# Fused conformer, MLP and attention kernel: the second pointwise product and the first MLP chunk by block of 128 tokens, and the last modulation vector as dot products inside the MLP

## The chip, the cores and the metric

One Trainium2 chip, one of its cores. The metric is the device time of one execution in microseconds. A difference of under about 0.2% (2 us) can't be told from no change for this kernel, as its three runs of before already lie 1.8 us apart.

## The reference, cut to what matters

The part of the program that is changed lies in the first block: conformer convolution, gated residual, modulated norm, squared-relu MLP, gated residual. x has 256 tokens of 1,024 channels; the MLP is 4,096 wide.

```python
mod = (silu(c) @ w_mod + b_mod)                      # six vectors of 1,024
sh1, s1, g1, sh2, s2, g2 = jnp.split(mod, 6, axis=-1)
# conformer_conv ends in:  u = silu(layer_norm(u)); y = u @ w_pw2 + b_pw2
xl = xl + g1 * y
hf = rms_norm(xl, norm2_g) * (1.0 + s2) + sh2
xl = xl + g2 * (jnp.square(jax.nn.relu(hf @ w1)) @ w2)
# second block: two attention layers with their own MLPs, then the last norm
```

The kernel numbers the six vectors in its own way: 0 and 1 are scale and shift of the first norm, 2 is g1, 4 and 3 are scale and shift of the second norm, 5 is g2.

## The kernel before

All products run in three passes of fp32r: each weight tile is split into a high part `hi` (ScalarE, L612) and a low part `lo` (VectorE, L1068), each activation likewise into `xh` and `xl` (or `gh` and `gl`), and TensorE adds high*high, low*high and high*low.

Weights come as one stream of units of 1 MB each, in a fixed order that `plan_units` writes out. SyncE's queue (SP) issues all of them, in that order, each into one of six slots of `raw` and `scratch`. A unit is issued when the unit six places before it has been consumed: a split unit when its `lo` is made, a modulation unit when its dot products or its products on TensorE are done. SP is one queue: an instruction that waits there holds back all that are behind it. The split parts have three slots, so `hi` of a unit waits until the product three units before it is done.

A modulation vector comes in four units (quarters) that are consumed in one of two ways. As dot products (`dots`, L1137), VectorE multiplies two halves of the unit with a row that holds silu(c), and sums. In the other way TensorE multiplies (`quarters`, L1757), ScalarE copies the result (`quarter_copy`, L669) and TensorE adds it up, into columns (`column_sums`, L1776) for scale and shift, or into a row (`row_sum`, L1788 and L1789, then `row_copy`, L677) for g2. `DOTS` says which units are dot products. g1, made of dot products, is a column; SP writes it to DRAM (L553) and reads it back as a row on all partitions (L556).

Names in what follows: the units in question are, in stream order, **28** and **29** (third quarters of vectors 4 and 3), **30** and **31** (their last quarters), **32** and **33** (the two halves of w1's first chunk), then in the kernel before the four quarters of g2, and then w1's second chunk. **24** and **27** are the last two units of the second pointwise product (pw2), whose splits are s=10 and s=11 in the code; the splits of 32 and 33 are s=12 and s=13.

The order of work on each engine is written out by hand; each engine runs its list in order. Before the change the stretch in question is, on VectorE: `lo` of 24, dot products of 29, `lo` of 27, dot products of 30 and 31, `lo` of 32, the gated residual in four pieces (block of 128 tokens by half of the channels; L1316 multiplies, L1319 adds), norm of block 0 (L1329), `lo` of 33, norm of block 1, the four low parts of the activation (L1278). The sum of squares is ScalarE's (L625), the root is GpSimd's (L1014, L1017). TensorE runs pw2 (`token_major` and `last_pw2`), then the four quarters of g2 with their row sums and, between them, the transposes of blocks 0 and 1 (`mid_T`, L1955), and then the MLP. Each of the MLP's eight chunks is a w1 product of 96 matmuls with the weights stationary and 256 tokens moving (L2007), whose result is the hidden layer already transposed, and a w2 product of 96 matmuls of 512 columns (L1652).

Of the kernel before, what the change touches and what calls it, by code (L numbers as in the profile page):

```python
# [14 lines left out]
P = 128  # L15
# [171 lines left out]
MOD_BANKS = [5] * GROUPS + [7, 6, 2, 3] + [0] * 4  # L187
SUM_AT = [(6, 0)] * GROUPS + [(3, QUARTER)] + [(6, 0)]
ROW_UNITS = (8, 9, 10, 11)
COLUMN_UNITS = ((None, 0), (None, 1), (None, 2), (None, 3), (4, 5), (6, 7))  # L190
# [5 lines left out]
def copies(m):  # L196

    return m + 1
# [25 lines left out]
ROWS = ("b_mod5", "b_pw2", "b_pw1a", "b_pw1g")  # L224
# [6 lines left out]
V_END = 10 * KT  # L231
# [5 lines left out]
def build(nc, stream, x, p_t, vectors, rows, rel, consts, dft_tables, taps, tap_bias, out):  # L237

    ctx = ExitStack()
    with ctx:  # L240
# [55 lines left out]
        def carve(table, start=0, limit=16512):  # L296
            views, at = {}, start
            for name, size in table:
# [6 lines left out]
                     ("stage", 4 * QUARTER), ("sel", P), ("sel1", 1), ("csb", KT * 32), ("g1", D), ("crow", D), ("dot", 2 * len(DOT_UNITS)), ("gate", KT),  # L305
# [18 lines left out]
        sq = one["yb"][:, 0:KT * SEQ].rearrange("p (f t) -> p f t", f=KT)  # L324
        hid1 = one["yb"][:, 0:NB * MLP_CHUNK].rearrange("p (b c) -> p b c", b=NB)
# [55 lines left out]
        gate_dram = nc.dram_tensor("gate_dram", (D,), F32, kind="Internal").ap()  # L381
# [8 lines left out]
        row_sums row_evac midT_ps mid_done mid_hi mid_lo xT_ps xh_ready xl_ready pw2_ps res_step relu_done  # L390
# [30 lines left out]
        def stage_free(eng, m):  # L421

            if m < 4:
                return
            old = m - 4
            if old in ROW_UNITS:
                eng.wait_ge(S["row_sums"], ROW_UNITS.index(old) + 1)
            else:
                eng.wait_ge(S["col_sums"], [old in g for g in COLUMN_UNITS].index(True) + 1)

# [10 lines left out]
        def nval(n, b):  # L441

            return 2 * WHOLE.index(n) + b + 1

# [55 lines left out]
        def _(sp):  # L500
# [31 lines left out]

            sp.dma_start(vec, vectors).then_inc(S["in_vec"], 16)
# [18 lines left out]
            sp.wait_ge(S["gate_done"], 1)  # L552
            sp.dma_start(gate_dram.rearrange("(p j) -> p j", p=P), one["gate"]).then_inc(S["gate_dma"], 16)  # L553
            sp.wait_ge(S["wave_ps"], CHUNKS)
            sp.wait_ge(S["gate_dma"], 16)
# [1981 lines left out]
```

## Time and profile before

| | |
|---|---|
| median of 3 runs | 1026.15 us (1024.49 to 1026.32) |
| profiled execution, its own time | 1025.7 us |
| its span, first to last instruction | 1023.8 us |
| TensorE busy (share of the span) | 992.0 us (97%) |
| VectorE, ScalarE busy | 618.1 us (60%), 503.9 us (49%) |
| mean granted TensorE clock | 0.993 of full |

The span is what the engines' rows add up to; the profiled execution's own time is 1.9 us longer. TensorE is busy nearly all the time, so that what counts is where it isn't, and what it waits for there.

### The profile page before, as it was taken

To read this page: it belongs to the slowest core of one execution; us is meant where nothing else is said; L and a number is where in the kernel's file an instruction comes from. 1 tells how busy PE (TensorE), PEld (TensorE's weight loads), DVE (VectorE), ACT (ScalarE), POOL (GpSimd) and SP (SyncE) were. 2 spreads that over 40 slices of the span, in tenths; PEclk is the share of its full clock that TensorE was granted. 3 is DMA by queue.
4 is the path that set the end of the run, shared out by engine and by line. 5 is a ranking of instruction groups with operands and counts; after the bars stand their busy time and mean duration, and the time that the engine had idled before them with its cause. 6 is when DMAs were issued, how large, how long until landed. Compare 5 with 4: busy or idle time off the path is not lost.

```text
span 1023.8 us, 13497 instructions
## 1 busy us (share of the span) xinstructions
PE 992.0 (97%) x5626; PEld 837.5 (82%) x5626; DVE 618.1 (60%) x748; ACT 503.9 (49%) x628; POOL 25.0 (2%) x47
## 2 busy tenths in 40 slices
PE   8999899999998999999999999999999999999996
PEld 6665689999987999878888888889987788888885
DVE  5786935444448649865455455664895654545465
ACT  4445365455454547644444444653664644443453
POOL 0000000000000000010000000100000100000010
PEclk9999899999999999999999999999999999999999
DMA  9987886654525443245555456435323555555531
GB/s 334 415 307 278 331 349 234 205 200 165 198 70 193 176 152 130 71 165 206 203 170 203 170 200 221 158 133 201 124 83 125 195 206 170 200 186 185 199 110 41
DMA packets 30934, 196.07 MB, mean 192 GB/s; under 512 B 3731, under 2 KB 5832, under 8 KB 9880
## 3 DMA queue, kind: packets, MB, share of 16 engines
q1 hardware_dynamic: 30874, 195.22, 52.6%
q8 instruction: 44, 0.72, 0.3%
q14 instruction: 16, 0.13, 0.0%
HBM read 194.14 MB, written 2.04 MB: 192 GB/s over the span
## 4 chain that ended last, share of the span: by engine, by line
PE 80%; DVE 12%; issue 3%; ACT 3%; DMA 2%; POOL 0%; SPq 0%; DVEq 0%; POOLq 0%; ACTq 0%
PE ps L1652 56%; PE ps L2007 9%; PE ps L2063 5%; DVE lo L1068 3%; ACT hi L612 1%; DMA scratch<-stream 1%; PE ps L1757 1%; PE ps L2311 1%; PE ps L2193 1%; PE ps L2147 1%; DVE scratch L1444 1%; DMA h<-x 1%; DVE scratch L1510 1%; DVE scratch L1461 1%; PE ps L2214 0%
## 5 line engine op out<-in xcount | busy, mean ns | idle before, releaser
L1068 DVE TENSOR_TENSOR lo<-raw,hi 128x2048 fp32r<-128x2048 f32 (+5 forms) x140 | 310.3, 2219 | 232.1 <-ACT hi L612 232.1
L612 ACT ACTIVATE hi<-raw 128x2048 fp32r<-128x2048 f32 (+4 forms) x140 | 263.8, 1888 | 143.1 <-PE ps L1652 110.1
L1652 PE MATMUL ps<-hi,xh 128*128 128x512 f32 (+2 forms) x704 | 275.1, 391 | 10.0 <-DVE xl L1109 4.4
L1652 PE MATMUL ps<-lo,xh 128*128 128x512 f32 (+2 forms) x704 | 269.2, 382 | 0.0
L1652 PE MATMUL ps<-hi,xl 128*128 128x512 f32 (+2 forms) x704 | 268.9, 382 | 0.0
L1652 PEld LDWEIGHTS ps<-hi,xh 128*128 128x128 f32 x704 | 132.2, 188 | 45.0 <-issue 11.1
L1652 PEld LDWEIGHTS ps<-lo,xh 128*128 128x128 f32 x704 | 132.1, 188 | 25.1
L1652 PEld LDWEIGHTS ps<-hi,xl 128*128 128x128 f32 x704 | 132.4, 188 | 22.6
L1652 PE MATMUL ps<-hi,gh 128*128 128x512 f32 (+2 forms) x328 | 125.2, 382 | 0.0
L1652 PE MATMUL ps<-lo,gh 128*128 128x512 f32 (+2 forms) x328 | 124.6, 380 | 0.0
L1652 PE MATMUL ps<-hi,gl 128*128 128x512 f32 (+2 forms) x328 | 124.5, 380 | 0.0
L2007 PE MATMUL ps<-xh,hi 128*128 128x256 f32 x256 | 72.6, 284 | 0.8 <-DVE xl L1278 0.8
L2007 PE MATMUL ps<-xh,lo 128*128 128x256 f32 x256 | 72.4, 283 | 0.0
L2007 PE MATMUL ps<-xl,hi 128*128 128x256 f32 x256 | 72.4, 283 | 0.0
L1652 PEld LDWEIGHTS ps<-hi,gh 128*128 128x128 f32 x328 | 61.6, 188 | 11.5 <-issue 0.7
L1652 PEld LDWEIGHTS ps<-lo,gh 128*128 128x128 f32 x328 | 61.6, 188 | 11.4
L1652 PEld LDWEIGHTS ps<-hi,gl 128*128 128x128 f32 x328 | 61.6, 188 | 10.8
L2063 PE MATMUL ps<-xh,hi 128*128 128x256 f32 x192 | 55.3, 288 | 0.9 <-DVE lo L1068 0.7
L2063 PE MATMUL ps<-xl,hi 128*128 128x256 f32 x192 | 54.3, 283 | 0.0
L2063 PE MATMUL ps<-xh,lo 128*128 128x256 f32 x192 | 54.3, 283 | 0.0
L2007 PEld LDWEIGHTS ps<-xh,hi 128*128 128x128 f32 x256 | 49.1, 192 | 1.7 <-issue 1.3
L2007 PEld LDWEIGHTS ps<-xl,hi 128*128 128x128 f32 x256 | 49.1, 192 | 0.2
(257 smaller groups left out, 1062.8 us busy)
## 6 DMA issues: line engine op xcount, KB each, us to landing
raw<-stream SPq DMA_DIRECT2D x142, 1024.0 KB, 4.8
scratch<-stream SPq DMA_DIRECT2D x22, 1024.0 KB, 8.9
raw<-stream SPq DMA_DIRECT2D x4, 1020.0 KB, 5.0
raw<-stream SPq DMA_DIRECT2D x4, 896.0 KB, 4.9
raw<-stream SPq DMA_DIRECT2D x2, 864.0 KB, 4.5
raw<-stream SPq DMA_DIRECT2D x2, 768.0 KB, 5.1
raw<-stream SPq DMA_DIRECT2D x2, 680.0 KB, 5.1
h<-x SPq DMA_DIRECT2D x2, 512.0 KB, 5.3
```

What stands on the lines that cost most here:

```text
L612: nc.scalar.activation(hi[:, u["s"] % SPLIT_SLOTS, 0:n], raw_of(u, n), ACT.Copy).then_inc(S["hi_done"], 1)
L1068: nc.vector.tensor_tensor(lo[:, slot, first:n], raw_of(u, n)[:, first:n], hi[:, slot, first:n].bitcast(F32), ALU.subtract).then_inc(S["lo_ ...
L1444: nc.vector.scalar_tensor_tensor(out=work[b], in0=r[:, k, :], scalar=iw[:, b, head:head + 1], in1=in1, op0=ALU.mult, op1=ALU.add).then_inc ...
L1461: nc.vector.match_replace(work[b], top8[:, b, :], work[b], TAKEN).then_inc(S["topk_step"], 1)
L1510: nc.vector.tensor_scalar(pm[b][:, hh, :], pm[b][:, hh, :], row_inv[:, c:c + 1], None, ALU.mult).then_inc(S["m_norm"], 1)
L1652: ins = nc.tensor.matmul(out, l, r, start=start and i == 0, stop=stop and i == 2, skip_group_check=skip)
L1757: ins = nc.tensor.matmul(ps[32 * j:32 * j + 32, MOD_BANKS[m], 0:QUARTER], csb[:, k, :], w[:, k, :], start=step == 0, stop=step == 1)
L2007: ins = nc.tensor.matmul(out_, w[:, k, cs], a[:, kk, :], start=(kk == 0 and c % 2 == 0 and i == 0), stop=(kk == KT - 1 and i == 2), skip_g ...
L2063: ins = nc.tensor.matmul(ps[:, bank + c // 2, (c % 2) * SEQ:(c % 2 + 1) * SEQ], w[:, k, cs], a[:, kk, :], start=(kk == 0 and c % 2 == 0 an ...
L2147: nc.tensor.matmul(ps[:, bank, at % 512:at % 512 + nk], qT[0:QK, hh, b * P:(b + 1) * P], kT[0:QK, hh, 0:nk], start=True, stop=False, skip_ ...
L2193: ins = nc.tensor.matmul(ps[:, bank, dst], w, sbt[:, hh, src], start=False, stop=True, skip_group_check=True)
L2311: ins = nc.tensor.transpose(ps[:, 6 + b, k * P:(k + 1) * P], hid2[:, b, k * P:(k + 1) * P], ident)
```

## The change

1. `DOTS` loses the last quarters of vectors 4 and 3 (units 30 and 31, now products on TensorE with column sums, the seventh group of `COLUMN_UNITS`) and gains all four of g2. g2's quarters move from ahead of the MLP's second chunk into chunks 1 to 4, one in each, as dot products; the result goes through DRAM like g1's. Row sums, row copies and their constants go away.
2. SP: the write of g1 no longer stands right ahead of its read. Units 28 to 31 are issued between the two.
3. pw2's last two units run as a `closing_pair`: block 0, then block 1, and ahead of its last six matmuls TensorE runs the quarters of 30 and 31 and the transposes of block 0.
4. Residual, sum of squares (now in halves), norm, scale and shift and the splits of the activation are written block by block. The first four channel groups of a block are ScalarE's, the last four VectorE's (`mid_second`).
5. The first w1 chunk is token major: 48 matmuls of 512 columns, block 0 and then block 1, with `mid_T(1)` between. Its result isn't transposed, so that eight transposes of the hidden layer (`first_hidden_T`) are added in the second chunk.

```diff
-DOTS = {(0, 0), (0, 1), (0, 2), (0, 3), (2, 0), (2, 1), (2, 2), (2, 3), (4, 2), (3, 2), (4, 3), (3, 3)}
+DOTS = {(0, 0), (0, 1), (0, 2), (0, 3), (2, 0), (2, 1), (2, 2), (2, 3), (4, 2), (3, 2), (5, 0), (5, 1), (5, 2), (5, 3)}
...
-    mod(5, 0, 1, 2, 3)
     for j in range(MLP_CHUNKS + 1):
         if 0 < j < MLP_CHUNKS:
             add("w1", j, [4, 4], MLP_CHUNK)
+        if 0 < j <= GROUPS:
+            mod(5, j - 1)
...
+            gate_write(0)
+            at, end = end, units_of("w1", 0)[0]["index"]
+            weights(UNITS[at:end])
+            gate_read(0, one["g1"])
...
+            def mid_high(b):
+
+                act.wait_ge(S["midT_ps"], b + 1)
+                if b == 0:
+                    act.wait_ge(S["pw2_ps"], 2)
...
+                sl = slice(b * P, (b + 1) * P)
+                for i in range(KT // 2):
+                    pair = slice(2 * i, 2 * i + 2)
+                    if i < 2:
+                        for f in (2 * i, 2 * i + 1):
+                            nc.scalar.activation(full[:, f, sl], ps[:, 4 + 2 * b, f * P:(f + 1) * P], ACT.Identity, scale=in_scale[:, KT + f:KT + f + 1],
+                                                 bias=in_shift[:, KT + f:KT + f + 1]).then_inc(S["mid_own"], 1)
+                        act.wait_ge(S["mid_own"], 4 * b + 2 * (i + 1))
+                    else:
+                        act.wait_ge(S["mid_full"], 4 * b + 2 * (i - 1))
+                    nc.scalar.activation(xh[:, pair, sl], full[:, pair, sl], ACT.Copy).then_inc(S["mid_hi"], 1)
+
+            mid_squares(0)
             feed(units_of("w1", 0)[1], 0)
-            squares(1, 0)
             quarter_copy(8)
...
             quarter_copy(9)
...
+            mid_high(0)
+            mid_squares(1)
+            mid_high(1)
...
+            mid_residual(0, 0)
+            mid_residual(0, 1)
+            mid_norm(0)
+            mid_residual(1, 0)
+            scale_columns(7)
+            shift_columns(7)
+            dve.wait_ge(S["scale_done"], 2 * GROUPS)
+            dve.wait_ge(S["shift_done"], 2 * GROUPS)
+            mid_second(0)
+            mid_low(0, 0, 1, 2, 3)
+            mid_residual(1, 1)
+            feed(units_of("w1", 0)[1], 0)
+            mid_norm(1)
+            mid_second(1)
+            mid_low(1, 0, 1, 2, 3)
             for j in range(MLP_CHUNKS):
                 feed(last_of("w1", j))
+                if 0 < j <= GROUPS:
+                    dots(5, j - 1)
...
+            def last_quarters():
+
+                quarters(8)
+                quarters(9)
+                mid_T(0)
...
+            closing_pair(units_of("pw2")[2:4], xh, xl, lambda ins: ins.then_inc(S["pw2_ps"], 1), KT - 1, last_quarters)
+            column_sums(6)
...
+            def mid_waits(u, b):
+
+                pe.wait_ge(S["mid_lo"], 4 * b + 2 * u["part"] + 2)
...
+            token_major(units_of("w1", 0), xh, xl, [slice(0, MLP_CHUNK)], lambda b, i: ps[:, b, :],
+                        done=lambda ins: ins.then_inc(S["w1_ps"], 1), waits=mid_waits, together=(2,), between=second_mid_T)
```

VectorE, from `lo` of unit 27 to the first low parts of the activation. Before:

```order
L1068 TENSOR_TENSOR lo<-raw,hi 128x2048
L1137 SCALAR_TENSOR_TENSOR raw,scratch<-raw,scratch 128x1024 x4
L1152 TENSOR_TENSOR scratch<-scratch 128x2
L1155 TENSOR_TENSOR scratch<-scratch 128x2
L1170 TENSOR_TENSOR scratch<-scratch 128x2
...
L1068 TENSOR_TENSOR lo<-raw,hi 128x2048
L1316 TENSOR_TENSOR xs<-ps,scratch 128x512
L1319 TENSOR_TENSOR h<-xs,h 128x512
...
L1329 TENSOR_SCALAR xs<-h,rstd 128x1024
L1068 TENSOR_TENSOR lo<-raw,hi 128x2048
L1329 TENSOR_SCALAR xs<-h,rstd 128x1024
```

And in the changed kernel, from `lo` of unit 32 (L1106 is the line of all `lo`, L1357 and L1360 are the residual's two steps, L1370 is the norm, L1189 to L1208 the scale and shift columns, L1376 `mid_second`, L1386 `mid_low`):

```order
L1106 TENSOR_TENSOR lo<-raw,hi 128x2048
L1357 TENSOR_TENSOR xs<-ps,scratch 128x512
...
L1370 TENSOR_SCALAR xs<-h,rstd 128x1024
L1357 TENSOR_TENSOR xs<-ps,scratch 128x512
L1360 TENSOR_TENSOR h<-xs,h 128x512
L1189 TENSOR_TENSOR scratch<-ps,scratch 128x2
...
L1376 TENSOR_SCALAR scratch<-ps,scratch 128x128 x4
L1386 TENSOR_TENSOR xl<-scratch,xh 128x2x128 x4
L1357 TENSOR_TENSOR xs<-ps,scratch 128x512
L1360 TENSOR_TENSOR h<-xs,h 128x512
L1106 TENSOR_TENSOR lo<-raw,hi 128x2048
L1370 TENSOR_SCALAR xs<-h,rstd 128x1024
```

The four dot-product instructions of units 30 and 31 are gone from here. Both `lo` of w1's first chunk keep their place in the list, the first ahead of every residual piece, the second now behind the last residual piece and behind all of block 0's activation.

SP, from the issue of g1's write. Before:

```order
L553 DMA gate_dram<-scratch 128x8
L556 DMA scratch<-gate_dram 128x1024
L515 DMA scratch<-stream 128x2048 x2
L515 DMA raw<-stream 128x2048 x4
```

And in the changed kernel:

```order
L537 DMA gate_dram<-scratch 128x8
L516 DMA scratch<-stream 128x2048 x2
L516 DMA raw<-stream 128x2048 x2
L543 DMA scratch<-gate_dram 128x1024
L516 DMA raw<-stream 128x2048 x2
L519 DMA gain<-row_final_g 128x1024
```

The read of g1 (0.5 MB) has moved behind units 28 to 31 and stands now right ahead of units 32 and 33.

## Rows read from the trace of the kernel before

**Rows 1.** Windows: busy time by engine, granted clock, DMA share and GB/s.
```profile
92.00:96.00 4.00, 4.00 (x52) 2.98 (x50) 1.08 (x4) 2.76 (x6) 0.00 (x0) 1.00 0.97 281
127.00:130.00 3.00, 3.00 (x26) 1.87 (x18) 2.29 (x2) 0.54 (x2) 2.16 (x2) 0.63 1.01 355
120.15:135.24 15.09, 11.42 (x91) 5.89 (x90) 9.72 (x13) 8.27 (x16) 2.93 (x4) 0.77 1.01 413
```

**Rows 2.** Timeline of TensorE, 119 to 136 us: start, time, engine, line, what.
```profile
119.76 0.39 PE L1652 MATMUL ps<-lo,xh 128*128 128x512 f32 x1
122.48 1.94 PE L1757 MATMUL ps<-scratch 128*32 128x256 f32 x16 [2.33 <-DMA scratch<-stream]
128.43 1.44 PE L1955 MATMUL ps<-table,xs 128*128 128x128 f32 x8
131.55 1.09 PE L1955 MATMUL ps<-table,xs 128*128 128x128 f32 x8
135.24 0.36 PE L2007 MATMUL ps<-xh,hi 128*128 128x256 f32 x1 [0.85 <-DVE xl L1278]
```

**Rows 3.** The chain that ended last, 140 us on: start, time, what.
```profile
141.22 0.43 PE ps L1788 x2
141.96 17.47 PE ps L2007 x144
159.43 10.91 PE ps L1652 x48
```

**Rows 4.** Timeline of VectorE, 103 to 131 us.
```profile
103.72 0.16 DVE L1152 TENSOR_TENSOR scratch<-ps,scratch 128x2 f32<-128x2 f32 x1
104.06 2.28 DVE L1068 TENSOR_TENSOR lo<-raw,hi 128x2048 fp32r<-128x2048 f32 x1
118.10 2.29 DVE L1068 TENSOR_TENSOR lo<-raw,hi 128x2048 fp32r<-128x2048 f32 x1 [1.38 <-ACT hi L612]
120.31 0.68 DVE L1316 TENSOR_TENSOR xs<-ps,scratch 128x512 f32<-128x512 f32 x1
122.36 0.69 DVE L1319 TENSOR_TENSOR h<-xs,h 128x512 f32<-128x512 f32 x1
126.28 2.29 DVE L1068 TENSOR_TENSOR lo<-raw,hi 128x2048 fp32r<-128x2048 f32 x1
129.28 0.75 DVE L1329 TENSOR_SCALAR xs<-h,rstd 128x1024 f32<-128x1024 f32 x1 [0.71 <-POOL rstd L1017]
```

**Rows 5.** Timeline of ScalarE: `hi` of unit 32, and the first pair.
```profile
116.15 1.92 ACT L612 ACTIVATE hi<-raw 128x2048 fp32r<-128x2048 f32 x1 [11.25 <-DMA raw<-stream]
132.68 1.02 ACT L745 ACTIVATE scratch<-ps,scratch 128x256 f32<-128x256 f32 x2 [0.61 <-PE ps L1955]
```

**Rows 6.** SP: timeline of its issues, then its waits (total, times, longest).
```profile
91.12 0.33 SPq L556 DMA_DIRECT2D scratch<-gate_dram  x1
106.37 4.82 SPq L515 DMA_DIRECT2D raw<-stream  x4
...
SPq L555 <- DMA gate_dram<-scratch: 6.3, 1, 6.3
```

**Rows 7.** Groups by form: busy, mean ns of one, idle before.
```profile
L631 ACT ACTIVATE scratch<-h 128x512 f32<-128x512 f32 x12 | 7.6, 631 | 9.2 <-DVE h L1357 4.9 <-DVE h L1374 4.3
L877 ACT ACTIVATE scratch<-ps,neg_max 128x128 f32<-128x128 f32 x12 | 4.3, 406 | 0.0
L967 ACT ACTIVATE gh<-ps 128x256 fp32r<-128x256 f32 x40 | 13.2, 381 | 65.9 <-PE ps L2311 65.9
L1564 DVE TENSOR_SCALAR scratch<-scratch,row_inv 128x128 f32<-128x128 f32 x10 | 2.1, 283 | 0.1
L1606 DVE TENSOR_TENSOR gl<-ps,gh 128x256 fp32r<-128x256 f32 x40 | 15.1, 420 | 28.5 <-ACT gh L967 28.5
L1137 DVE SCALAR_TENSOR_TENSOR raw<-raw,scratch 128x1024 f32<-128x1024 f32 x20 | 23.6, 1220 | 1.0 <-DMA raw<-stream 0.9
```

**Rows 8.** Timeline of VectorE in an MLP chunk.
```profile
186.14 2.29 DVE L1068 TENSOR_TENSOR lo<-scratch,hi 128x2048 fp32r<-128x2048 f32 x1 [5.71 <-ACT hi L612]
```

More of the change, by code:

```diff
@@ L324, in build @@
         sq = one["yb"][:, 0:KT * SEQ].rearrange("p (f t) -> p f t", f=KT)
+        full = one["u"].rearrange("p (k t) -> p k t", k=KT)
         hid1 = one["yb"][:, 0:NB * MLP_CHUNK].rearrange("p (b c) -> p b c", b=NB)
@@ L424, in stage_free @@
                 return
[L425 to L429, printed above, removed]
+            eng.wait_ge(S["col_sums"], [m - 4 in g for g in COLUMN_UNITS].index(True) + 1)
         NORMS = 3 + 3 * LAYERS + 1
@@ L759, in _, with mid_squares @@
             feed(units_of("w1", 0)[0], 0)
+            def mid_squares(b):
+                for c in range(2):
+                    if c == 0:
+                        act.wait_ge(S["res_step"], 3 * b + 2)
+                    else:
+                        act.wait_ge(S["h_ready"], hval(1, b))
+                    cs = slice(c * CHUNK, (c + 1) * CHUNK)
+                    nc.scalar.activation(xs[:, b, cs], h[:, b, cs], ACT.Square, scale=D ** -0.5,
+                                         accum_out=half_ss[:, 2 * b + c:2 * b + c + 1]).then_inc(S["sumsq"], 1)
@@ L1325, in _, with mid_residual @@
-            for b in range(NB):
-                if b:
-                    feed(units_of("w1", 0)[1], 0)
+            def mid_residual(b, c):
+                at = 2 * b + c
+                if at < 3:
+                    dve.wait_ge(S["pw2_ps"], at + 1)
+                else:
+                    product(dve, "pw2")
+                cs = slice(c * CHUNK, (c + 1) * CHUNK)
+                nc.vector.tensor_tensor(xs[:, b, cs], ps[:, at, :], one["g1"][:, cs], ALU.mult).then_inc(S["res_step"], 1)
+                rstep[0] += 1
+                dve.wait_ge(S["res_step"], rstep[0])
+                ins = nc.vector.tensor_tensor(h[:, b, cs], xs[:, b, cs], h[:, b, cs], ALU.add)
+                if c == 0:
+                    ins.then_inc(S["res_step"], 1)
+                    rstep[0] += 1
+                else:
+                    ins.then_inc(S["h_ready"], 1)
@@ new lines, in mid_low @@
+            def mid_low(b, *pairs):
+                sl = slice(b * P, (b + 1) * P)
+                for i in pairs:
+                    dve.wait_ge(S["mid_full"], 4 * (b + 1))
+                    dve.wait_ge(S["mid_hi"], KT // 2 * b + i + 1)
+                    pair = slice(2 * i, 2 * i + 2)
+                    nc.vector.tensor_tensor(xl[:, pair, sl], full[:, pair, sl], xh[:, pair, sl].bitcast(F32), ALU.subtract).then_inc(S["mid_lo"], 1)
+            dve.wait_ge(S["gate_dma"], 32)
+            mid_residual(0, 0)
@@ L1936, in pw2_waits @@
                     column_sums(5)
-            def last_pw2(b):
-                u = last_of("pw2")
-                pw2_waits(u, b)
-                wh, wl = parts(u)
-                sl = slice(b * P, (b + 1) * P)
-                for i, c in enumerate(halves):
-                    for k in range(u["kts"]):
-                        kk = u["k0"] + k
-                        ins = three(ps[:, 2 * b + i, :], xh[:, kk, sl], xl[:, kk, sl], wh[:, k, c], wl[:, k, c], start=False,
-                                    stop=kk == KT - 1)
-                    ins.then_inc(S["pw2_ps"] if 2 * b + i < 3 else S["used"], 1)
             def mid_T(b):
@@ L1989, in w2_product @@
                     used(ins, u)
-            for j in range(MLP_CHUNKS):
+            for j in range(1, MLP_CHUNKS):
                 if j >= 2:
```

207 lines of the change are left out of this document (92 added, 115 removed).

## The prediction

> **What bounds the kernel now.** I read the windows first: from 120.15 to 135.24 us, between the last matmul of pw2 and the first of the MLP, TensorE is busy for 11.42 of 15.09 us at a granted clock of 0.77 [rows 1], and none of it is work of the large products. Then the timeline of TensorE [rows 2]: the last pw2 matmul starts at 119.76 and is through at 120.0, a wait of 2.33 us for a DMA follows (the first quarter of g2), then quarters, row sums and transposes, and the first w1 matmul starts at 135.24 after a wait for VectorE. From there the chain is TensorE alone [rows 3]: 144 matmuls of 256 columns in 17.47 us (0.121 each), 48 of 512 columns in 10.91 us (0.227 each). The row sum and its step at 141.22 cost 0.74 us (the next piece starts at 141.96). So the first w1 chunk ends at 141.96 + 48 x 0.121 = 147.8, and behind it TensorE has no gap in the MLP. All that the change can win or lose lies between 120.0 and 147.8, and in what it adds to TensorE behind that.
>
> What sets the order in that stretch is not TensorE. ScalarE waits 11.25 us for unit 32 and starts `hi` at 116.15 [rows 5]; VectorE's `lo` follows at 118.10, the first residual piece at 120.31 [rows 4]. So all of the residual hangs on the landing of unit 32. The stream is in turn held by VectorE: SP issues unit 30 at 106.37 [rows 6], right when `lo` of unit 24 (104.06 + 2.28 = 106.34) [rows 4] has freed its slot.
>
> **Step 1, the landing of unit 32.** The wait for g1's write, 6.3 us on SP [rows 6], goes away, and units 28 and 29 can be issued somewhat earlier. I cost this at nothing: the next issue, unit 30, waits for `lo` of 24, and that `lo` waits for a column sum on TensorE (the scale column at 103.72) [rows 4], neither of which moves. But g1's read, which at 91.12 fell in idle time of the queues, now stands between 31 and 32. It is 0.52 MB in a stream that leaves no gap, for which I take the rate of the full stretch in rows 1, 413 GB/s: 1.25 us. The trace shows such reads dearer. With g1's read under way the rate is 281 GB/s over 4 us (92 to 96), 4 x (413 - 281) / 413 = 1.3 us lost beside its own 1.25, together 2.6, part of which is the start of the queue; with a gain row of the same size it is 355 over 3 us (127 to 130), 0.4 lost, together 1.7 [rows 1]. I take 1.9, nearer to the row inside a running stream; bounds 1.25 and 2.6. `hi` of 32 then starts at 118.05, `lo` at 120.0, the first residual piece at 122.2.
>
> The Trainium skill's page "DMA: Bandwidth & Descriptors" (Where 436 GB/s comes from) has the ports' ceiling at 435 GB/s and gives no penalty for a row that is read 128 times over. By it alone the read would cost 1.2 us and the sum below would be 0.7 lower; the two windows speak against it.
>
> **Step 2, TensorE up to the norm of block 0.** pw2's matmuls are the same in number. All but the last six (6 x 0.227 = 1.4) are done by 118.7, or 0.4 later, as block 0 alone needs `lo` of 27 sooner; the quarters of 30 and 31 take about 1.0 each at full clock (half of 1.94, which was at half clock) [rows 2]. TensorE is free at 121.1 and waits for the norm of block 0. On VectorE a residual piece takes 1.35 us (from 120.31 to the second piece's add, which ends at 123.05, it is 2.74 for two) [rows 4]: both are through at 124.95. Half a sum of squares is 0.63 on ScalarE [rows 7] and 0.1 more to read it out; GpSimd's small step, 0.3 by the usual size of such steps, and its root follow, for which VectorE waited 0.71 [rows 4]: about 1.75 in all; the norm takes 0.75 [rows 4]. The transposes can start at 127.5. TensorE has then been idle for 6.4 us, with pw2's last six matmuls queued behind the wait.
>
> **The clock.** In the trace 2.33 us of idleness were followed by half clock, 1.2 GHz: 16 quarter matmuls took 1.94, eight transposes 1.44 against 1.09 at full clock [rows 2]. After 6.4 us I expect half clock too: transposes to 128.8, six matmuls of 512 columns at twice 0.227 to 131.4, column sums to 132.2. At full clock all this would be 1.7 us shorter.
>
> The page "TensorE: Matmul & The Clock Gate" (Part 1, HAM oscillation) says that idleness between bursts puts the array back to half rate and that only sustained matmuls lift it again. The trace agrees for the fall. By that rule block 0's product, in pieces with waits between, might stay slow; that is a rival below, priced from rows.
>
> **Step 3, block 0's activation.** Behind the column sums VectorE makes the last scale and shift columns (0.34, from 103.72 to 104.06) [rows 4] and starts `mid_second` at 132.8. It and `mid_low` are not in the trace. For 128x128 with two operands I take 0.22 each, the nearest row (L1564, 0.283) less the usual overlap of 0.07; for 128x256 from L1606 (0.42) 0.34 each [rows 7]. Four and two: low parts for w1's first half at 134.5, all four at 135.1. The first w1 matmul thus starts at 134.55, hardly before the old 135.24. The half-product is 12 x 0.227 = 2.7, to 137.3.
>
> **Step 4, the second `lo`.** It was hidden under the transposes at 126.28 [rows 4]. Now it comes behind the last residual piece: 135.1 + 1.35 + 2.25 = 138.7. Block 0's second half waits 1.4 us for it and ends at 141.5. The norm of block 1 stands behind that `lo` and is done by some 140.2, hidden by this half.
>
> **Step 5, block 1.** Transposes 141.5 to 142.5. Nothing is left to cover the evacuation: ScalarE makes two 128x128 pieces and one 128x256 copy for each pair. At 0.33 to 0.4 and 0.38 [rows 7] a pair is 1.1 us; as a floor, half of the old pair's two (1.02 for two of 256 columns) [rows 5] with the copy gives 0.85, and as a ceiling the old pair unchanged, 1.6. Two pairs and one low part: 2.7, floor 2.2, ceiling 3.7. TensorE starts at 145.3, and 24 x 0.227 = 5.45 end the chunk at 150.8. The product itself is 10.9 instead of 11.5.
>
> **Step 6, the rest.** Eight transposes more in chunk 2: 1.0 at full clock [rows 2]. g2 costs VectorE 2 x 1.22 = 2.4 us in each of four chunks [rows 7]; they fall in the 5.7 us that VectorE is idle each chunk [rows 8]. Without this cover it would be up to 2.4 x 4 = 9.8. In the first of them `hi` and `lo` of w2's first unit (1.9 + 2.3) come behind the hidden transposes and have 5.8 us of w1's second half: enough, with 0.2 to 0.4 to spare after the copies. g2's write and read stand where SP has nothing urgent; all that is small at the start (one copy less) is nothing.
>
> **Sum.** 150.8 - 147.8 = 3.0, plus 1.0, is +4.0; I add 0.1 for the chance that the clock is back later. Against the profiled execution's own 1025.7 that is 1029.8; the median of the runs is 0.45 above it, so 1030.2.
>
> **Rivals.**
> - *The clock stays down through block 0's product.* For it: waits at 132.2 and 137.3 break up what TensorE has. Against: the old rise came while it did small pieces (0.63 mean in 127 to 130) [rows 1]. Block 0's halves would take 5.5 each instead of 2.7: the first ends at 140.0, past the second `lo`, the second at 145.5 instead of 141.5: 1034.
> - *The small terms fall low.* g1's read at its full rate (-0.65), six matmuls and what stands round them at full clock (-1.7), evacuation at its floor (-0.5): the first two together give 1027.9, all three 1027.3.
> - *The released SP decides (the other side).* If what paces the stream were g1's 6.3 us wait and not `lo` of unit 24, units 30 to 33 would land up to 6.3 earlier, and with them the residual: 1030.2 - 6.3 = 1023.9. It decides from a gain of 6.1 on. For it: VectorE's dot products of unit 28 had to wait for that load. Against: 106.37 follows 106.34 on the dot.
> - *A split in chunks 1 to 4 comes late* because the dot products stand ahead of `lo` units: each 0.5 us late in four chunks gives +2, 1032. Against: 5.7 us idle for 2.4 of work.
>
> **How the numbers follow.** My sum 0.52 (own range 1028.6 to 1032), clock down 0.13, small terms 0.18 (half of it above 1028.2), released SP 0.07, late splits 0.10. The range, 1027.4 to 1034, leaves out the released SP (0.07), half of the clock case (0.06), 0.03 of the small terms and 0.02 of the late splits. The bounds of step 1 and 5 alone (-0.65 to +0.7, -0.5 to +1.0) give 1029 to 1032. With 2 us as what can be told: slower by more 0.84 (all but half of the small terms and the released SP), within 0.09, faster 0.07.
>
> **What would show it.** Right: g1's read ahead of unit 32 and `hi` of 32 some 2 us later; TensorE idle for about 6 us ahead of block 0's transposes, then half clock; a wait of 1 to 2 us for `lo` inside block 0's product, one of 2 to 3 us ahead of block 1's; no gap in chunks 2 to 8. It would be wrong if unit 32 doesn't land later, if the first w1 matmul starts much before 134, or if gaps appear in the later chunks.

## The result, and the profile after

The changed kernel takes 1035.14 us, the median of four runs (1033.13 to 1037.01); the kernel before took 1026.13 beside it (1024.49 to 1026.32). The ratio is 1.0093, 95% interval [1.0081, 1.0105]: slower by 0.9%, where +0.4% was predicted. The predicted 1030.2 and its range, 1027.4 to 1034.0, are both too low. The profiled execution is the quickest of the four, 1033.13 us, with a span of 1031.3 (before 1023.8) and a mean granted clock of 0.990 (0.993). So 7.5 us of the difference can be read in the trace.

SP's timeline (start, time) has the issues where the prediction put them: units 30 and 31, g1's read, units 32 and 33.

```profile
106.90 0.80 SPq L516 DMA_DIRECT2D raw<-stream  x2
107.82 0.36 SPq L543 DMA_DIRECT2D scratch<-gate_dram  x1
108.22 3.50 SPq L516 DMA_DIRECT2D raw<-stream  x2
```

ScalarE's timeline has `hi` of unit 32 at 120.04, where [rows 5] has 116.15:

```profile
120.04 1.91 ACT L629 ACTIVATE hi<-raw 128x2048 fp32r<-128x2048 f32 x1 [14.61 <-DMA raw<-stream]
```

From the first of these issues it is now 13.14 us, before it was 9.78 [rows 5, 6]: the landing is 3.36 us later. The other 0.53 of the 3.89 is from the kernel's start (unit 30 is issued at 106.90 instead of 106.37, g1's write is 0.53 later too). The windows (columns as in [rows 1], GB/s last) show the stretch from the issue of unit 30 to `hi` of 32, before and then in the changed kernel; then, in the changed kernel, a slow stretch of the stream, and the stretch from the quarters to the first w1 matmul:

```profile
106.37:116.15 9.78, 9.78 (x45) 8.09 (x44) 9.30 (x15) 0.00 (x0) 0.00 (x0) 1.00 0.88 358
```

```profile
106.90:120.04 13.14, 12.88 (x59) 10.03 (x61) 4.77 (x8) 0.00 (x0) 0.00 (x0) 1.00 0.93 348
114.00:116.00 2.00, 2.00 (x10) 1.65 (x10) 0.00 (x0) 0.00 (x0) 0.00 (x0) 1.00 0.97 297
119.81:137.86 18.05, 7.35 (x56) 5.72 (x55) 9.60 (x18) 9.36 (x18) 0.86 (x2) 0.71 0.80 334
```

From the issue of unit 30 to `hi` of 32 the queues moved 358 GB/s x 9.78 us = 3.50 MB before, and now 348 x 13.14 = 4.57 MB. Of the 1.07 MB more the read is 0.52; the other 0.55 MB isn't the read's, so data from behind unit 32 moved before unit 32 was whole. A rate doesn't show that part (1.3 us at 413 GB/s).

From the quarters to the first w1 matmul TensorE is busy for 7.35 of 18.05 us, at 0.71 of its clock (before 11.42 of 15.09 at 0.77, [rows 1]). Its timeline, to be held against [rows 2]:

```profile
119.81 1.93 PE L1835 MATMUL ps<-raw,scratch 128*32 128x256 f32 x32
129.58 1.97 PE L2003 MATMUL ps<-table,xs 128*128 128x128 f32 x8 [7.83 <-DVE xs L1370]
131.20 0.78 PE L1728 MATMUL ps<-hi,xh 128*128 128x512 f32 x1
131.77 0.63 PE L1728 MATMUL ps<-hi,xl 128*128 128x512 f32 x1
...
133.91 1.08 PE L1854 MATMUL ps<-scratch 128*128 128x1 f32 x8
137.86 0.76 PE L1728 MATMUL ps<-hi,xh 128*128 128x512 f32 x1 [2.87 <-DVE xl L1386]
...
144.90 1.03 PE L2003 MATMUL ps<-table,xs 128*128 128x128 f32 x8
148.96 0.50 PE L1728 MATMUL ps<-hi,xh 128*128 128x512 f32 x1 [3.02 <-DVE xl L1386]
```

Three waits stand where [rows 2] has 2.33 and 0.85: 7.83 us for block 0's norm, 2.87 for its low parts, 3.02 for block 1's. Behind the first, TensorE works at half clock (1.2 GHz): eight transposes in 1.97, matmuls of 512 columns every 0.43 us. The granted clock is back at 1.00 from 134.2, is 0.50 again from 137.6, just ahead of the first w1 matmul, and 1.00 from 141.0. VectorE's timeline shows what they wait for:

```profile
121.98 2.29 DVE L1106 TENSOR_TENSOR lo<-raw,hi 128x2048 fp32r<-128x2048 f32 x1 [10.28 <-ACT hi L629]
124.19 0.68 DVE L1357 TENSOR_TENSOR xs<-ps,scratch 128x512 f32<-128x512 f32 x1
...
128.77 0.75 DVE L1370 TENSOR_SCALAR xs<-h,rstd 128x1024 f32<-128x1024 f32 x1 [1.84 <-POOL rstd L1055]
...
135.03 0.16 DVE L1189 TENSOR_TENSOR scratch<-ps,scratch 128x2 f32<-128x2 f32 x1 [4.17 <-PE ps L1854]
...
135.55 1.37 DVE L1376 TENSOR_SCALAR scratch<-ps,scratch 128x128 f32<-128x128 f32 x4
136.95 1.43 DVE L1386 TENSOR_TENSOR xl<-scratch,xh 128x256 fp32r<-128x256 f32 x4
...
139.62 2.28 DVE L1106 TENSOR_TENSOR lo<-raw,hi 128x2048 fp32r<-128x2048 f32 x1
```

At 135.03 VectorE has waited 4.17 us for the last column sums, which stand behind block 0's transposes and the six held-back matmuls. The chain from there (start, time), against [rows 3]:

```profile
137.86 7.21 PE ps L1728 x24
145.06 0.89 PE ps L2003 x8
...
148.96 5.76 PE ps L1728 x24
154.71 5.75 PE ps L2072 x48
160.47 0.87 PE ps L2025 x8
161.34 5.75 PE ps L2072 x48
167.09 10.91 PE ps L1728 x48
177.99 11.51 PE ps L2072 x96
```

The first w1 chunk ends at 154.71, before it was 147.8. Behind it there is no gap in the MLP in either kernel: +0.87 for the transposes of the hidden layer, and g2's dot products are hidden. The chunk ends 6.9 us later, and with the 0.87 that is 7.8, where the span is 7.5 longer: but for these transposes and the 0.53 of the start, all of the loss is made between 107 and 155 us.

### The profile page after: what moved, and what is told of

Its sections match the earlier page's. It is cut to its first block, busy times and chain, and to the rows that moved or that the text cites. A ratio compares the mean times of both kernels' runs of the same rounds, so it can differ in the third digit from the quotient of the medians.

```text
span 1031.3 us, 13372 instructions
## 1 busy us (share of the span) xinstructions
PE 988.1 (96%) x5550; PEld 835.7 (81%) x5550; DVE 625.8 (61%) x768; ACT 501.8 (49%) x630; POOL 25.0 (2%) x47
## 4 chain that ended last, share of the span: by engine, by line
PE 72%; DVE 10%; issue 2%; ACT 2%; DMA 0%; POOL 0%; DVEq 0%; POOLq 0%; ACTq 0%
PE ps L1728 53%; PE ps L2072 8%; PE ps L2124 5%; DVE lo L1106 3%; ACT hi L629 1%; PE ps L2372 1%; PE ps L2254 1%; PE ps L2208 1%; DVE scratch L1520 1%; DVE scratch L1586 1%; DVE scratch L1537 1%; PE ps L2275 0%; DVE h L1343 0%; DMA raw<-stream 0%; DVE xs L1138 0%
## 5 line engine op out<-in xcount | busy, mean ns | idle before, releaser
L1106 DVE TENSOR_TENSOR lo<-raw,hi 128x2048 fp32r<-128x2048 f32 (+5 forms) x140 | 310.3, 2220 | 230.3 <-ACT hi L629 230.2
L1728 PE MATMUL ps<-hi,xh 128*128 128x512 f32 (+2 forms) x720 | 283.3, 394 | 15.8 <-DVE xl L1386 5.9
L1728 PE MATMUL ps<-lo,xh 128*128 128x512 f32 (+2 forms) x720 | 276.4, 384 | 0.0
L1728 PE MATMUL ps<-hi,xl 128*128 128x512 f32 (+2 forms) x720 | 276.2, 384 | 0.0
L1728 PEld LDWEIGHTS ps<-hi,xh 128*128 128x128 f32 x720 | 136.0, 189 | 52.0 <-issue 13.0
L1728 PEld LDWEIGHTS ps<-hi,xl 128*128 128x128 f32 x720 | 136.3, 189 | 23.2
L2072 PE MATMUL ps<-xh,hi 128*128 128x256 f32 x224 | 63.4, 283 | 0.0
L2072 PE MATMUL ps<-xh,lo 128*128 128x256 f32 x224 | 63.4, 283 | 0.0
L2072 PE MATMUL ps<-xl,hi 128*128 128x256 f32 x224 | 63.4, 283 | 0.0
L2124 PE MATMUL ps<-xh,hi 128*128 128x256 f32 x192 | 55.3, 288 | 0.9 <-DVE lo L1106 0.7
L2124 PE MATMUL ps<-xl,hi 128*128 128x256 f32 x192 | 54.3, 283 | 0.0
L2124 PE MATMUL ps<-xh,lo 128*128 128x256 f32 x192 | 54.3, 283 | 0.0
L985 ACT ACTIVATE scratch<-ps,rstd 128x256 f32<-128x256 f32 x44 | 20.8, 473 | 55.4 <-PE ps L1728 55.4
L1001 ACT ACTIVATE gh<-ps 128x256 fp32r<-128x256 f32 x40 | 13.2, 382 | 66.2 <-PE ps L2372 66.2
```

The costliest lines, as they stand in the source:

```text
L985: nc.scalar.activation(silu2[:, b, :], ps[:, gate_bank(j, b), 0:FF_CHUNK], ACT.Silu, scale=scale).then_inc(S["silu_g"], 1)
L1001: nc.scalar.activation(dst[:, 0:2, b * P:(b + 1) * P], ps[:, 6 + b, 0:2 * P].rearrange("p (k m) -> p k m", k=2), ACT.Copy).then_inc(S["gh_ ...
L1106: nc.vector.tensor_tensor(lo[:, slot, first:n], raw_of(u, n)[:, first:n], hi[:, slot, first:n].bitcast(F32), ALU.subtract).then_inc(S["lo_ ...
L1728: ins = nc.tensor.matmul(out, l, r, start=start and i == 0, stop=stop and i == 2, skip_group_check=skip)
L2072: ins = nc.tensor.matmul(out_, w[:, k, cs], a[:, kk, :], start=(kk == 0 and c % 2 == 0 and i == 0), stop=(kk == KT - 1 and i == 2), skip_g ...
L2124: ins = nc.tensor.matmul(ps[:, bank + c // 2, (c % 2) * SEQ:(c % 2 + 1) * SEQ], w[:, k, cs], a[:, kk, :], start=(kk == 0 and c % 2 == 0 an ...
```

## The experiments

Fourteen experiments. Each time is a median, and the ratio is to the kernel before, measured beside it on the same chip (its median there was 1025.65 in the first four, 1025.93, 1025.78 and 1026.07 in the others). The lines of the edits are those of the functions named in the diff above.

**1. g1's read ahead of unit 30** (the change with this edit):

```diff
-            at, end = end, units_of("w1", 0)[0]["index"]
+            at, end = end, units_of(("mod", 4), 3)[0]["index"]
             weights(UNITS[at:end])
             gate_read(0, one["g1"])
```

> The changed kernel, with g1's read issued between units 29 and 30 (when the queues are idle) and not between 31 and 32. Theory L (landing): the read ahead of unit 32 makes it land 3.4 us later, and all of the residual hangs on that; without it, hi of unit 32 starts near 117 instead of 120.04 and the kernel takes 3.0 to 3.5 us less than the changed kernel's median, about 1031.8. Rival O (order and clock): the loss lies behind the residual, in what TensorE waits for and at what clock; then a landing 3 us sooner is eaten by a longer wait elsewhere and the kernel stays within 1 us of 1035.

Measured: 1031.82 us (1028.30 to 1034.20), ratio 1.0052 [1.0032, 1.0071]. `hi` of 32 starts 9.81 us after the first issue (106.29), as before the change:

```profile
116.10 1.92 ACT L629 ACTIVATE hi<-raw 128x2048 fp32r<-128x2048 f32 x1 [11.27 <-DMA raw<-stream]
```

Block 1's product begins at 144.39 instead of 148.96: 0.61 of that is the start of this execution, 3.33 the landing, the rest the clock (block 0's transposes take 1.72 us here). The median is 3.3 us below the change's: the place of the read costs what the trace said.

**2. The kernel before, with its read moved behind unit 31** (the same move alone, the write stays).

> The kernel before, with nothing changed but the place of g1's read: behind units 28 to 31, as in the change. Theory L: unit 32 lands 2.5 to 3.4 us later here too, and the kernel takes 1028.6 to 1029.5. Rival O: before the change VectorE has other work there and TensorE its quarters, so that most is hidden: 1026 to 1027.

Measured: 1029.14 us, ratio 1.0035 [1.0025, 1.0045]; `hi` of 32 at 119.25, 13.11 us after the first issue. The late read alone makes the kernel before some 3.5 us slower, as theory L had it.

**3. TensorE kept busy in its idle time** (the change, with 28 matmuls whose result nobody reads):

```diff
                 quarters(9)
+                for _ in range(28):
+                    nc.tensor.matmul(ps[:, 5, 384:512], neg_ones[:], neg_ones[:], start=True, stop=True)
                 mid_T(0)
```

> The changed kernel, with 28 matmuls of 128x128 on constants (7 us at full clock, their result is never read) in the gap of 7.8 us ahead of block 0's transposes, to keep the clock up. Theory C (clock): the transposes, the last six pw2 matmuls and the column sums take 3.3 instead of 5.4 us, block 0's product runs at full clock, minus 2 to 3 us in all, and the runs lie closer together than 1033 to 1037: 1032.5. If the clock is only a symptom, the time stays at 1035 within 1 us, since the wait for the second lo takes up what the product gains.

Measured: 1030.65 us, ratio 1.0053 [1.0035, 1.0071]. TensorE's timeline:

```profile
121.67 6.52 PE L2011 MATMUL ps<-neg_ones 128*128 128x128 f32 x56
129.59 1.09 PE L2003 MATMUL ps<-table,xs 128*128 128x128 f32 x8 [1.40 <-DVE xs L1370]
...
131.90 0.95 PE L1854 MATMUL ps<-scratch 128*128 128x1 f32 x8
135.72 0.77 PE L1728 MATMUL ps<-hi,xh 128*128 128x512 f32 x1 [2.87 <-DVE xl L1386]
```

The transposes start where they did (129.58), but take 1.09 instead of 1.97, and at the first w1 matmul 2.1 us are won. That product is slow at its start all the same, as in the change, behind the wait of 2.87 us; of the 13.6 us of half clock between 118 and 152 us, 3.4 are left. The median fell by 4.5 us, more than the 2 to 3 of the theory and than the 2.5 between the two profiled executions.

**4. The last six pw2 matmuls and the column sums ahead of block 0's transposes**, and ScalarE's quarter copies ahead of its squares:

```diff
                 quarters(9)
-                mid_T(0)
...
             column_sums(6)
+            mid_T(0)
```

> The changed kernel, with the last six matmuls of pw2 and the column sums ahead of block 0's transposes and no longer behind them, and the two quarter copies on ScalarE ahead of the squares. Theory O (order): VectorE needn't wait 4.17 us for the column sums, mid_second of block 0 starts at about 131.5 instead of 135.55, and the kernel takes 3.5 to 4 us less, about 1031.3. Theory L alone: the residual is where it was, and little changes, 1034 to 1035, because the second lo and block 1 then set the time.

Measured: 1031.68 us, ratio 1.0055 [1.0038, 1.0072]. The column sums are through by 123.4. Block 1's product begins at 145.40, 3.6 us earlier, of which 0.9 is the start of this execution (`hi` of 32 is at 119.15): 2.7 us by the trace, 3.5 by the medians. The hold was a loss of the change's order of work. (The quarter copies, which the column sums need, were moved with it; neither was tried without the other.)

**5. The change again, unaltered**, with the three kernels that follow.

> The whole change once more, unaltered, on the same chip as the three kernels beside it. If the 1033.1 to 1037.0 us of the first measurement are its ordinary spread, its median here lies between 1033 and 1036. If that chip was a poor sample, it lies near 1032, the span that its profiled execution explains.

Measured: 1035.47 us (1033.6 to 1036.04), ratio 1.0086 [1.0072, 1.0101]. The profiled execution is again the quickest, 1033.6. Its chain:

```profile
135.82 8.29 PE ps L1728 x24
...
148.00 7.32 PE ps L1728 x24
```

Both blocks' products, not only block 0's, begin at half clock here: in this trace 17.0 us of half clock lie between 118 and 152 us, in the first trace 13.6, in that of before 6.8 (time at a granted clock of 0.50). How much of the stretch is slow differs from execution to execution.

**6. Only the fifth vector moved** (the kernel before; g2's units in chunks 1 to 4 as dot products, no quarters, row sums or row copies; residual, norm, transposes and the first chunk stay whole).

> The kernel before, with only the fifth modulation vector moved: its four units stand in MLP chunks 1 to 4 and are summed as dot products, the four quarter products and row sums leave the pointwise end and the MLP. The product itself stays whole, for both blocks. Theory (the vector's part is a gain, the split by block is the loss): the second block's transposes start when its norm ends (130.0 instead of 131.5), and the row sum between the two halves of chunk 0 (0.74 us with its gap) is gone: -2.2 us, against which TensorE may be slow for up to 1 us more, having less to do; 1024.0 to 1025.3 us. Rival (the vector's dots in the MLP cost something that the trace does not show, such as DMA order or VectorE time): 1026 us or more.

Measured: 1026.11 us, ratio 1.0002 [0.9993, 1.0011]. No gain. TensorE's timeline:

```profile
126.64 1.94 PE L1938 MATMUL ps<-table,xs 128*128 128x128 f32 x8 [6.48 <-DVE xs L1325]
130.22 1.97 PE L1938 MATMUL ps<-table,xs 128*128 128x128 f32 x8 [1.64 <-DVE xs L1325]
134.78 0.55 PE L1980 MATMUL ps<-xh,hi 128*128 128x256 f32 x1 [2.59 <-DVE xl L1274]
135.13 0.41 PE L1980 MATMUL ps<-xl,hi 128*128 128x256 f32 x1
```

The second transposes start 1.3 us earlier than in [rows 2], as expected, but take 1.97 instead of 1.09, and the first w1 matmuls come every 0.21 instead of 0.12. With the quarters gone TensorE idles for 6.48 us, and 13.7 us at half clock follow. The first w1 matmul comes 0.46 us earlier (134.78 for 135.24), and the row sum inside the chunk (0.84 from its start to the next w1 matmul) is gone; but the second half of the chunk begins at 141.88, for 141.89 before. So what was saved, 1.3 us, went into the slow first half. From there on the pieces of the chain in chunks 1 to 4 are as long as before (11.51 and 10.91 us), so the rival's cost of the dot products isn't there.

**7. Edits 1 and 4 together.**

> The change, with the read of g1 ahead of unit 30's transfer and with the last six product matmuls and the column sums ahead of block 0's transposes (both of the edits tried singly). The two causes are independent in the theory: -3.3 us by the landing and -3.5 us less what the half clock takes differently, so block 1's first matmul at about 141.5 instead of 148.96 and 1027 us by the profiled execution. Rival (the six matmuls only waited because the landing was late, so the two gains overlap): 1028.5 to 1030 us.

Measured: 1028.20 us, ratio 1.0020 [1.0011, 1.0029]; block 1's product begins at 142.59. Of the 9.5 us between the change (experiment 5) and the kernel before, 7.3 are undone; one by one the edits gave 3.3 and 3.5. In the trace block 1's product begins 6.37 us earlier: 0.46 is the start, 3.30 the landing, which leaves 2.6 for the hold, where it gave 2.7 alone. So the two causes add up, though the median lies 1.2 us above the theory's 1027 and just below the rival's range.

**8. The same with 24 matmuls in the idle time.**

> The same with 24 matmuls of 128x128 whose result nobody reads between the last product matmuls and block 0's transposes, to keep TensorE busy in its idle time. Theory (part of the loss is the half clock after the idle time): transposes in 1.1 us instead of 2.0 and the first product at full speed, 1.5 to 2 us less than the kernel without them: 1025 to 1026 us. Rival (with the landing early the gap is short enough, and what ends the wait is VectorE): no difference within 0.5 us.

Measured: 1030.00 us, ratio 1.0038 [1.0025, 1.0051]. Mis-sized: they took 5.60 us in an idle time of 2.1, and block 0's transposes began at 128.75 instead of 125.82. The transposes ran at full clock (1.04 us), and the clock was 0.50 again from 133, behind a wait of 3.11 us. What a fill that fits is worth it doesn't tell.

**9. The same with 9 matmuls.**

> The kernel with the early read and without the hold (1028.2 us), with 9 matmuls of 128x128 before block 0's transposes instead of the 24 that had delayed them by 3 us: 18 records of 0.114 us, 2.1 us in an idle time of 2.3. Theory (keeping TensorE busy pays here as it did in the change itself): transposes in 1.1 us instead of 2.0, block 0's product at full speed, 1026 to 1027.3 us. Rival (the clock falls anyway in the 3.1 us behind the transposes, as it did with 24): 1 us at most is won, 1027.3 to 1028.2 us.

Measured: 1028.03 us, ratio 1.0023 [1.0014, 1.0033]. TensorE's timeline:

```profile
125.70 1.10 PE L2003 MATMUL ps<-table,xs 128*128 128x128 f32 x8
129.91 0.47 PE L1728 MATMUL ps<-hi,xh 128*128 128x512 f32 x1 [3.11 <-DVE xl L1386]
134.02 0.50 PE L1728 MATMUL ps<-hi,xh 128*128 128x512 f32 x1 [1.14 <-DVE lo L1106]
...
142.38 0.63 PE L1728 MATMUL ps<-lo,xh 128*128 128x512 f32 x1
```

Now block 0's product is at full speed, and so it waits 1.14 us for the second `lo`, the wait that the prediction's step 4 had; the half clock falls on block 1's product instead. Even so the first w1 chunk ends at 148.11, for 149.54 in kernel 7. But the two profiled executions differ by 0.45 us only (1027.75 and 1028.20): at the end of the MLP ScalarE waits for the landing of a unit of the next stage, and waits 1.0 us longer. Its timeline in kernel 7, and then in kernel 9:

```profile
307.98 1.91 ACT L629 ACTIVATE hi<-raw 128x2040 fp32r<-128x2040 f32 x1 [2.87 <-DMA raw<-stream]
```

```profile
307.55 1.91 ACT L629 ACTIVATE hi<-raw 128x2040 fp32r<-128x2040 f32 x1 [3.87 <-DMA raw<-stream]
```

So the fill gained 1.4 us in this stretch, and that landing took 1.0 of it.

**10. Block 1's transposes inside block 0's product** (kernel 7 with this edit; `midway` is called ahead of a unit's third block of rows):

```diff
-                if u["part"] == 0 and b == 1:
+                if u["part"] == 1 and b == 0:
...
-                        ..., together=(2,), between=second_mid_T)
+                        ..., together=(2,), midway=second_mid_T)
```

> The kernel with the early read and without the hold (1028.2 us), and in it block 1's eight transposes stand in the middle of the second half of block 0's product instead of behind it, so that block 1's evacuation goes on beside six matmuls. Theory (what is left of the loss is the idle time between the two blocks' products, 3.0 us, and the half clock behind it, 1.4 us): the transposes follow block 1's norm, which ends at 136.5, the evacuation ends at 140.5, so block 1's product begins 2.1 us earlier, and perhaps at full speed: 1024.8 to 1026.2 us. Rival (the transposes now wait inside the product and TensorE goes slow anyway): 1027.5 to 1028.5 us.

Measured: 1025.30 us, ratio 0.9997 [0.9988, 1.0005]: no different from before, and in the theory's range. TensorE's timeline has the last wait at 1.64 instead of 3.02 us, and no half clock behind it:

```profile
137.96 1.04 PE L2005 MATMUL ps<-table,xs 128*128 128x128 f32 x8
138.75 0.48 PE L1728 MATMUL ps<-hi,xh 128*128 128x512 f32 x1
...
142.02 0.50 PE L1728 MATMUL ps<-hi,xh 128*128 128x512 f32 x1 [1.64 <-DVE xl L1386]
```

**11 and 12. The read itself** (the change; for half the read both halves of the residual use the same 512 columns, for other rows 128 rows of x stand in g1's place):

```diff
-                sp.dma_start(dst, gate_dram[g].partition_broadcast(P))...
+                sp.dma_start(one["g1"][:, 0:CHUNK], gate_dram[0][0:CHUNK].partition_broadcast(P))...   # 11
+                sp.dma_start(one["g1"], x[0:P, :])...                                                 # 12
```

> The whole change, but the read of g1 fetches only the first 512 columns for each partition (256 KB instead of 512), which both halves of the residual then use; the output is wrong by that. What the read costs the units behind it was 3.4 us. If the cost goes by bytes, unit 32's hi starts 1.7 us earlier than in the change (about 118.4) and the time falls by 1.7 us. If it is a cost of having a read there at all (a wait, a restart of the stream), it stays within 0.5 us.

> The whole change, but the read of g1 takes 128 different rows of x (512 KB in pieces of 4096 bytes, as before) instead of 128 times the same row of gate_dram; the output is wrong by that. If the same 4 KB read 128 times are what is slow, unit 32's hi starts 1 to 2 us earlier (118 to 119) and the time falls as much. If it is the size and the pieces, nothing changes within 0.5 us.

Measured: 1033.27 us, ratio 1.0074 [1.0060, 1.0088], for half the read; 1030.78, ratio 1.0056 [1.0043, 1.0070], for other rows. `hi` of 32, first with half the read, then with other rows:

```profile
117.58 1.91 ACT L631 ACTIVATE hi<-raw 128x2048 fp32r<-128x2048 f32 x1 [13.11 <-PE ps L1730]
```

```profile
117.66 1.92 ACT L631 ACTIVATE hi<-raw 128x2048 fp32r<-128x2048 f32 x1 [12.50 <-DMA raw<-stream]
```

The first row names a matmul, but in experiment 1 the same matmuls had let `hi` go at 116.10, so I take it for the landing, which is argued. From the first issue (105.93 and 106.63) to `hi`, and over the 9.78 of before:

| read between units 31 and 32 | issue to `hi` | cost |
|---|---|---|
| none there (before; experiment 1) | 9.78; 9.81 | 0 |
| one row of 4 KB, 128 times (the change; experiment 2) | 13.14; 13.11 | 3.4; 3.3 |
| its first half, 128 times | 11.65 | 1.9 |
| 128 different rows of 4 KB | 11.03 | 1.25 |

The cost of the repeated row goes about by its bytes, and 128 different rows cost just what 0.52 MB take at the stream's 413 GB/s [rows 1]. The same row 128 times costs 2.7 times that. (The source tensor changes with the rows in experiment 12; a tensor of its own with 128 copies wasn't tried.) The bytes moved up to `hi` of 32 are 3.98 MB with other rows (361 GB/s x 11.03 us), the read's own 0.5 more than before and no others; in experiment 2 they are 4.60 (351 x 13.11), as in the change. With half the read the median is 1.9 us below the change's, as the theory had it; the profiled execution, the slowest of its four (1034.45), had 23.9 us of half clock. With other rows it is 4.4 us below, twice the 2.1 by which unit 32 lands earlier; the profiled execution had 10.2 us of half clock, where the change had 13.6.

**13 and 14. The idle time filled in the best of both forms**: kernel 10 with 9 matmuls, kernel 6 with 22 and 5.

> The per-block form with all three edits (early read, no hold, block 1's transposes inside the product), with 9 matmuls of 128x128 in the 2.1 us ahead of block 0's transposes. Theory (half clock is what is left): transposes 0.9 us shorter, first six to twelve product matmuls at full speed, but block 1's transposes still follow its norm (136.5), so at most 1 us of it reaches the end: 1024.2 to 1025 us. Rival (the norm of block 1 and the evacuation set the end, so TensorE's speed before them is hidden): 1025.3 us within 0.4.

> The kernel before with only the fifth modulation vector moved (1026.1 us on an earlier chip, no gain), with 22 matmuls of 128x128 in the 6.5 us ahead of block 0's transposes and 5 in the 1.6 us ahead of block 1's. Theory (its gain was eaten by the half clock: 13.7 us of it, against 6.8 before): block 1's transposes take 1.1 instead of 2.0 us and the first 13 matmuls of the chunk 0.12 instead of 0.21 each, 2.1 us in all: 1023.6 to 1024.4 us, faster than before. Rival (no gain was there to be eaten, the dots cost it in the MLP): 1025.5 to 1026.5 us.

Measured: 1025.23 us in both, ratios 0.9992 [0.9983, 1.0001] and 0.9993 [0.9984, 1.0001]. Neither beats before by more than can be told. Kernel 13 lies where its rival had it, kernel 14 between its theory and its rival. In kernel 14 the transposes are fast, but the fall comes one step later, and the chunk ends 0.6 us earlier than before; its timeline of TensorE:

```profile
130.41 1.10 PE L1938 MATMUL ps<-table,xs 128*128 128x128 f32 x8 [1.46 <-DVE xs L1325]
134.10 0.36 PE L1984 MATMUL ps<-xh,hi 128*128 128x256 f32 x1 [2.59 <-DVE xl L1274]
...
135.21 0.42 PE L1984 MATMUL ps<-xl,hi 128*128 128x256 f32 x1
```

In kernel 13 block 1's product begins at 139.61, 2.4 us ahead of kernel 10, and the MLP's last w1 product ends as much earlier; then ScalarE waits for the same landing as in experiment 9. Its timeline in kernel 13, and then in kernel 10:

```profile
304.97 1.91 ACT L629 ACTIVATE hi<-raw 128x2040 fp32r<-128x2040 f32 x1 [4.21 <-DMA raw<-stream]
```

```profile
305.99 1.91 ACT L629 ACTIVATE hi<-raw 128x2040 fp32r<-128x2040 f32 x1 [2.79 <-DMA raw<-stream]
```

Of 2.4 us 1.0 is left: 1.4 us are given back at that landing, where the wait was 2.79 us. (0.75 of the 2.4 is the earlier start of that execution.) So it wasn't what the rival names, block 1's norm and evacuation, that hid the gain.

## Why the prediction was right and where it was wrong

The direction was right, and so were the places but one: the wait for `lo` inside block 0's product didn't come (step 4). No rival decided; that of the clock has the nearest number, 1034, but by a product that stays slow throughout, which it didn't. What failed is the size of terms in the sum, above all two: the landing in step 1 (+1.46 us) and the step from the profiled execution to the median (+1.5); the rest are five of 0.25 to 0.7, which all fell on the same side, against 0.13 that step 6 gave back. By its own steps, against the trace of the change (predicted start of block 1's product 145.3, measured 148.96, 3.66 later):

- **Step 1, the landing: the step that failed.** 1.9 predicted, 3.36 measured, outside the bounds of 1.25 and 2.6 (+1.46). I priced the read by the rate that the stream lost, and took the value near the gain row in a running stream, 1.7, although [rows 1] had the read of g1 itself as the dearer one; its 281 GB/s I put partly down to the start of the queue. Even the 2.6 from that window was too low as a ceiling. A lost rate leaves out that 0.55 MB from behind unit 32 went ahead of it, 1.3 us. Experiments 1 and 2 show the term from both sides; 11 and 12 show that it goes by the bytes of the repeated row and is gone with other rows (of another tensor). How the queues come to be held up is open: with half the read only the read's own 0.24 MB more were moved (321 GB/s x 11.65 us), and there it was the rate that fell. The page "DMA: Bandwidth & Descriptors" of the Trainium skill (Where 436 GB/s comes from) was weighed there with 1.2 us, from the ports' ceiling: for different rows that is near what was measured (1.25), for one row read 128 times it isn't (3.36). The prediction passed over the limit of about 358 GB/s that the same section has for reads from HBM; the stream here runs above it, at 413 [rows 1].
- **The released SP, and all rivals.** Nothing landed earlier: unit 30 was issued 0.53 later, with the whole kernel (+0.53). This start differs between executions of one kernel: unit 30 is issued at 106.90 here and at 105.77 in experiment 5.
- **Step 2, idle time and clock.** From `hi` to the transposes 9.54 us for 9.45, and half clock behind it, as predicted. From the transposes to `mid_second` 5.97 for 5.3 (+0.67): transposes 1.6, column sums 1.1 and two columns 0.5 instead of 1.3, 0.8 and 0.34. The 1.44 us from which the 1.3 was taken [rows 2] was not all at half clock: in that trace the granted clock is back at 1.00 from 129.2, in the middle of those eight; wholly at half clock they take 1.97. Experiment 3 shows what the clock costs there, 2.1 us, and experiment 4 what the order costs, 2.7 with a part of the same half clock in it.
- **Step 3, block 0's activation.** 2.31 instead of 1.75 (+0.56): `mid_second` takes 1.37 for four, 0.34 each, where I took 0.22 from an operation that doesn't read `ps`. The low parts (1.43 for four) and the start of w1 on the first two, 0.9 us behind, are as predicted.
- **Step 4, the second `lo`.** The mechanism was wrong, the number not: 7.04 us for 6.95. The product did not wait for `lo`; seven matmuls at half clock filled the same time. Experiment 9 shows the wait once the clock is up. That the number fits is luck. So it was partly the rival "the clock stays down", but for 3 us and not for the product: what came lies between the sum's case and that rival.
- **Step 5.** 4.06 from block 1's transposes to its product for 3.8 (+0.26), inside the bounds. 24 matmuls take 5.75, not 5.45 (0.24 each), and the chunk's end is 3.9 off where the product's start was 3.66 off.
- **Step 6.** 0.87 for 1.0; dots hidden, no late split.
- **From the profiled execution to the median.** I carried over 0.45 us; it is 2.0 (1035.14 to 1033.13), and 1.9 in experiment 5. The two traces have 13.6 and 17.0 us of half clock. The record has the mean granted clock of every execution: of the eight of the change, the four at 0.990 took 1033.13 to 1035.16 us, the four at 0.987 to 0.989 took 1035.78 to 1037.01; the six of experiment 1 go in order from 0.994 and 1028.30 to 0.986 and 1034.20. So the longer executions are those with more half clock. That it comes behind the same three waits in those without a trace is argued, not shown. This is 1.5 of the 4.9 us that the median was off.

What is left of the change once the read and the hold are put right is small: +0.20% (experiment 7), and with block 1's transposes inside the product nothing (experiment 10). The form by block is not worse as such; as I read the traces, what it overlaps had been covered already by the quarters of g2. Moving these away gains nothing either (experiment 6), as TensorE then idles and is slow afterwards; with the idle time filled it gains 0.6 us by the trace and by the medians nothing that can be told (experiment 14).

What stays open: why the clock fell behind some waits of 2.6 to 3.1 us, even after the idle time had been filled (experiments 3, 8, 13 and 14), and not behind others (block 0's wait of 3.11 in experiment 9).

## What to carry to other kernels

Look at what a DMA pushes back, not at what it moves: a broadcast row belongs where its queue is idle, and its price is to be read from a row of the same kind, source pattern included, and from the landing behind it rather than from a rate. When work is taken off an engine that is waiting anyway, ask what its clock does in the longer wait; here 1.3 us saved were paid back in full. A gain in one stretch can end at the next landing: 1.0 of 1.4 and 1.4 of 2.4 us did (experiments 9 and 13). And don't hold back work that others wait for behind a wait: the six matmuls and the column sums behind block 0's transposes cost 2.7 us.

## What the hardware showed that I had not expected

- Reading one 4 KB row for 128 partitions cost the stream 3.3 to 3.4 us, 128 different rows of the same size, from another tensor, 1.25 us.
- Filling an idle time with matmuls (experiments 3, 8, 9, 13, 14) kept the transposes behind it at full clock each time (1.04 to 1.10 us for eight), but the half clock then came after a later wait of 2.6 to 3.1 us: part of it was moved, not avoided. Less of it was left (3.4 us each in 3, 9, 13 and 14, where the same kernels without a fill had 10.2 to 13.7).
- `mid_second`, a scale and a shift of 128x128 from `ps` on VectorE, takes 0.34 us, and ScalarE's same step 0.4 (0.81 for two).
